# First row tiles in transfers of their own, first weights split behind the first roundings, and the next row's mean ahead of the last row's remainder

## What is computed

```python
xn = rmsnorm(x, norm1_g)            # x * rsqrt(mean(x*x) + EPS) * norm1_g
proj = xn @ w_in[0]                 # here: the q, k, v columns, 12 tiles of 128
qkv_c, new_buf = causal_conv(qkv, buf_qkv, conv_qkv_w)   # width 4, then SiLU
```

## Time and profile before

| | us |
|---|---|
| three runs, median | 1976.95 (1975.17 to 1980.42) |
| profiled execution, own time | 1980.5 |
| profiled execution, span | 1978.5 |

### The profile page before, as it was taken

One profiled execution on the slowest core, in us unless ns is written; L12 is line 12 of the kernel. 1 busy time (PEld: TensorE's weight loads), 2 busy tenths in 40 slices (PEclk: granted clock), 3 DMA queues, 4 the chain that ended last, 5 costly groups with the idle time before them and its releaser, 6 DMA issues. The chain is left out here.

```text
span 1978.5 us, 23341 instructions
## 1 busy us (share of the span) xinstructions
PE 1839.9 (93%) x10413; PEld 1727.8 (87%) x10413; DVE 724.1 (37%) x871; ACT 411.0 (21%) x590; POOL 98.1 (5%) x91
## 2 busy tenths in 40 slices
PE   5999799996799989979979989999999999999998
PEld 5999689995799989969977888989888898989887
DVE  5565566653311123222125333333333333333234
ACT  4233133330211011101113121111111111112021
POOL 1000233331000000000000000000000000000001
PEclk9999899998999989989999989999999999999999
DMA  5110100003021021121015011111111111111102
GB/s 175 33 33 22 47 1 1 1 7 85 12 77 40 0 54 44 32 65 37 27 46 188 1 44 43 54 32 54 32 54 32 47 39 43 43 43 43 43 11 96
DMA packets 109223, 88.08 MB, mean 45 GB/s; under 512 B 4010, under 2 KB 94839, under 8 KB 109132
## 3 DMA queue, kind: packets, MB, share of 16 engines
q1 hardware_dynamic: 109132, 86.72, 14.6%
HBM read 79.43 MB, written 7.28 MB: 44 GB/s over the span
## 5 line engine op out<-in xcount | busy, mean ns | idle before, releaser
L1891 PE MATMUL ps<-xn_hi,u_hi 128*128 128x384 f32 x768 | 258.7, 337 | 7.5 <-DVE u_lo L1773 5.5
L1891 PE MATMUL ps<-xn_lo,u_hi 128*128 128x384 f32 x768 | 258.2, 336 | 0.0
L1891 PE MATMUL ps<-xn_hi,u_lo 128*128 128x384 f32 x768 | 258.1, 336 | 0.0
L1900 PE MATMUL ps<-u_hi,hid_hi 128*128 128x512 f32 x576 | 226.5, 393 | 12.1 <-DVE hid_lo L1810 7.6
L1900 PE MATMUL ps<-u_hi,hid_lo 128*128 128x512 f32 x576 | 225.1, 391 | 0.0
L1900 PE MATMUL ps<-u_lo,hid_hi 128*128 128x512 f32 x576 | 224.9, 391 | 0.0
L1816 DVE TENSOR_TENSOR rows<-ps,rows 128x512 f32<-128x512 f32 x144 | 99.5, 691 | 245.0 <-PE ps L1900 245.0
L1891 PEld LDWEIGHTS ps<-xn_hi,u_hi 128*128 128x128 f32 x768 | 145.4, 189 | 8.2 <-DVE u_lo L1773 5.7
L196 PE MATMUL ps<-xn_hi,g_hi 128*128 128x384 f32 x384 | 130.4, 340 | 23.4 <-DVE g_lo L681 23.4
L196 PE MATMUL ps<-xn_hi,w_hi 128*128 128x384 f32 x384 | 130.7, 340 | 22.6 <-DVE w_lo L681 22.6
L1891 PEld LDWEIGHTS ps<-xn_lo,u_hi 128*128 128x128 f32 x768 | 145.6, 190 | 0.3
(11 more groups left out here) (250 smaller groups left out, 3029.4 us busy)
## 6 DMA issues: line engine op xcount, KB each, us to landing
w_raw<-in_w_up SPq DMA_DIRECT2D x32, 512.0 KB, 4.1
w_raw<-in_w_down SPq DMA_DIRECT2D x32, 512.0 KB, 3.8
w_raw<-in_w_in SPq DMA_DIRECT2D x28, 512.0 KB, 3.9
g_raw<-in_w_in SPq DMA_DIRECT2D x16, 512.0 KB, 4.5
rows<-in_x_prompt SPq DMA_DIRECT2D x9, 512.0 KB, 6.4
out<-out SPq DMA_DIRECT2D x9, 512.0 KB, 2.6
w_raw<-in_w_o SPq DMA_DIRECT2D x8, 512.0 KB, 4.4
rows<-in_x_prompt SPq DMA_DIRECT2D x2, 1024.0 KB, 10.1
```

The costliest lines, as they stand in the source:

```text
L1891: last = nc.tensor.matmul(ps[:, 3 * up_set(j) + g, 0:NW], y[:, j, w], x[:, k, x_at], start=(k == 0 and m == 0), stop=(k == KD - 1 and m == 2))
L1900: last = nc.tensor.matmul(ps[:, 6 + n % 2, :], x[:, k, r * P:(r + 1) * P], y[:, s, w], start=(k == 0 and m == 0), stop=(k == 3 and m == 2))
```

## The change

The rows' transfers are six instead of five: tiles 0, 1 and 2 each have their own. The order of issue becomes row tile 0, gain, row tile 1, the identity alone (`C_ONE` is column 128, `C_INC` column 256 of the table, so the transfer is half as large; the rest of the table, now from column 128, comes later as before), row tile 2, weight tile 0, row tiles 3 to 5, weight tile 1, and the rest as before. ACT's list has `split(0)` behind `square(3)` instead of ahead of `rounded(0)`, and `split(1)` behind `square(4)` instead of ahead of `rounded(1)`. DVE's list makes the mean of row tile r + 1 directly behind the scaling of row tile r, ahead of `left(r - 1)`; `rest(0)` moves from the round of r = 1 to that of r = 3, ahead of `left(2)`, and `rest(1)` from r = 2 to the end of the round of r = 4, behind `left(3)`. PE's and POOL's lists are as before.

```diff
-        X_GROUPS = ((0, 1), (1, 3), (3, 6), (6, 8), (8, 9))
+        X_GROUPS = ((0, 1), (1, 2), (2, 3), (3, 6), (6, 8), (8, 9))
...
                 load_x(0)
                 sp.dma_start(gain[:, :], norm1_g.to_broadcast([P, D])).then_inc(gain_in, 16)
-                sp.dma_start(self.con[:, 0:C_INC], table[:, 0:C_INC]).then_inc(ident_in, 16)
                 load_x(1)
+                sp.dma_start(self.con[:, 0:C_ONE], table[:, 0:C_ONE]).then_inc(ident_in, 16)
+                load_x(2)
                 load(0)
-                load_x(2)
+                load_x(3)
                 load(1)
-                load_x(3)
                 load_x(4)
+                load_x(5)
...
-                sp.dma_start(self.con[:, C_INC:C_END], table[:, C_INC:C_END]).then_inc(loaded, 16)
+                sp.dma_start(self.con[:, C_ONE:C_END], table[:, C_ONE:C_END]).then_inc(loaded, 16)
...
                 square(0)
                 square(1)
-                split(0)
                 rounded(0)
                 square(2)
-                split(1)
                 rounded(1)
                 square(3)
+                split(0)
                 rounded(2)
                 square(4)
+                split(1)
                 rounded(3)
...
+                mean_of(0)
                 for r in range(RT):
-                    mean_of(r)
                     scale(r)
-                    if r == 1:
+                    if r + 1 < RT:
+                        mean_of(r + 1)
+                    if r == 3:
                         rest(0)
-                    if r == 2:
-                        rest(1)
                     if r:
                         left(r - 1)
+                    if r == 4:
+                        rest(1)
                 left(RT - 1)
```

More of the change, by code:

```diff
@@ L226, in front @@
         v, alog, dtb, ea, gseq, egls = self.gate_tables()
-        x_in = self.sems(*(f"x_in{n}" for n in range(5)))
+        x_in = self.sems(*(f"x_in{n}" for n in range(6)))
         raw_ready = self.sems("raw_ready0", "raw_ready1")
```

## The result

The changed kernel takes **1981.05 us** (median of 12 executions, 1979.95 to 1981.99) where the kernel before, in the same comparison, takes 1976.72 (12 executions, 1975.17 to 1980.57): +4.3 us by the medians. The ratio is 1.0019 with a 95% interval of 1.001 to 1.0028, which is 3.8 us, the distance of the means (1981.10 and 1977.28). Medians and means part because the executions of before lie in groups, nine from 1975.2 to 1977.4 and three from 1980.0 to 1980.6. The change is a loss clear of noise, and under 0.3%. The forecast was 1981.5, +4.55.

A forecast was written before the change was run, and what follows sets the result against it. PE, busy 93% of the span, was taken as the bound. Waits of +2.85 us plus 1.7 for one clock fall gave +4.55: 1985.05 us against the profiled execution's 1980.5, a median of 1981.5, range 1976.7 to 1985.0.

The forecast's parts named there:

- The transfers: Start of the kernel: row tiles 3 to 5 still land at 15.6 us, bounds 15.2 and 16.1.
- the splitting: Weight splitting on ACT at the start: called hidden, as ACT finishes `rounded(1)` at about 14.3 us, then waits for row tile 3.
- The second weight tile: Ahead of `unit(1, 0)`: late `rest(1)` idles PE about 1.6 us; start at 32.8, early 1.8 us gone and 0.25 more.
- The wait for the square: Ahead of `unit(0, 1)`: `left(5)` queues behind a mean awaiting `square(7)`; PE idles 3.0 us, starting 2.45 us late at 41.15.
- The last turning: Turning of row tile 8: `left(6)` behind a mean awaiting `square(8)`; at 50.7, 2.85 us late, only 0.4 of it new.
- The clock: Ahead of `unit(0, 1)`: 3.0 us idle brings one fall to 1.2 GHz, costing 1.7 us; shorter idle times bring none.
- the step by idle length: PE's front idle times: 3.0 us judged by 3.75, 2.00 and 1.47 us neighbours, giving one fall; 1.6 and 1.4 none.
- The median: Whole kernel: 1981.5 us, from 1976.95 before, the profiled execution lying 3.5 us above that median.
- Rival B: Front of the kernel: the waits bite but the clock holds, +2.85 us or +1.9; chance 0.25.
- Rival C: More low clock ahead of `unit(1, 0)` or the last turning: +6.25 us with one more stretch, +7.95 with two; chance 0.17.
- D: The early start survives because `square(7)` comes early enough; last turning 1.8 us early; chance 0.05.
- E: Nothing reaches the end, 0 +- 1 us: late landing, waits in existing idle times, or a low-clock stretch falling away; chance 0.07.

## Why the prediction was right

**The transfers** did as worked out, slightly better. From the DMA views of the changed kernel (issue to landing), with SP's timeline:

```profile
rows<-in_x_prompt SPq DMA_DIRECT2D x1, 1536.0 KB, 11.5
...
2.11 0.43 SPq L277 DMA_DIRECT2D con<-in_table  x1
3.59 1.26 SPq L272 DMA_DIRECT2D rows<-in_x_prompt  x1
```

Row tiles 3 to 5 land at 3.59 + 11.5 = 15.1, not at 15.6 and just under the lower bound of 15.2. Hence the first product at 21.85 for 22.45. One remark fails: the splitting is not "hidden". It is so only in the sense that ACT then waits for row tile 3; with the old transfers and the same lists the first product was 1.9 us later.

**The second weight tile** was late by the mechanism named, with 1.77 us of idle time for 1.6. It came at 31.94, 0.85 us earlier than the 32.8 of the sum: 0.6 from the first product, the rest because PE was at full speed sooner (the turning of row tile 3, at 25.82, took 1.39 us for 1.60). That the first products run at the low clock is read from their pace, 0.32 us from start to start (24.54, 24.86, 25.18 in the changed kernel), as in the stretch at 1176.20; PEclk does not show it and reads 1.00 there:

```profile
22.00:26.50 4.50, 4.50 (x16) 4.40 (x17) 0.89 (x1) 0.00 (x0) 0.00 (x0) 1.00 0.88 290
```

Here the sum was mis-sized: it had the early start spent at this place, and 0.6 us of it was left.

**The wait for the square** is right to the place and the size: 3.00 us for 3.0, released by the remainder behind the mean. That the mean's place is the cause is shown by taking it back (-7 us against the changed kernel, the idle times down from 3.00 and 1.77 us to 1.23 and 0.15 us) and by making it alone (+4.7). The late weights add to it only where a mean holds `left(3)`. **The last turning** had an idle time of 1.21 us where 1.4 was expected.

**The clock** was right in number and wrong in place. One half-clock stretch was expected behind 3.00 us of idle time. In the first profile it stood behind 1.77 us, which the step had given none. It costs the same there, since nothing between the two takes it back: 51.43 is the forecast's 50.7 + 1.7 = 52.4 less the microsecond by which the first two terms were too large. So the step by idle length fails. Its neighbours were read rightly; these are the windows behind the idle times of 3.75 and 1.47 us in the kernel before:

```profile
1920.30:1923.80 3.50, 3.50 (x10) 2.71 (x10) 1.13 (x1) 0.00 (x0) 0.00 (x0) 0.51 0.48 150
1064.90:1068.00 3.10, 3.10 (x18) 2.71 (x19) 2.39 (x4) 2.01 (x4) 0.00 (x0) 1.00 1.08 342
```

But over all 14 profiles the clock fell behind the 3.75 us in 14, behind the 2.00 us in 13 and behind the 1.47 us in none, where it fell behind the 3.00 us in three of six and behind the 1.77 us in one of two: 3.00 us had it less often than 2.00 us. That idle times in the front bring it at all is likely: of the six profiles with one of 3.00 us four have a fall there, of the eight without none. What decides in the single case stays open.

The words of the Trainium skill (TensorE: Matmul & The Clock Gate, section HAM oscillation), that waits between bursts bring the lower clock back, hold for some of these idle times only; the waits for transfers in its example are mostly longer. What its section What's actually happening says of the start, that the number of slow matmuls differs from run to run, the runs now show: the turning of row tile 3 took 1.60 us and 1.04 us in the two profiles of before.

**The median** agrees to 0.5 us, in part by luck. The sum's own figure, 1985.05 for the profiled execution, was not met: it took 1981.2, next to its median, and the 3.5 us by which the first profile of before lay above its median belonged to that one execution. Taking them off was right. At the last turning the change costs 3.6 us against one profile of before and 4.2 against the other, where the sum has 4.55. The rest of the 4.3 may come from the stretch near 88 us, 1.6 us, that both profiles of the changed kernel have and one of two of the kernel before; the prediction had counted it as neutral. Rival B (the clock holds) does not fit: both profiles have a fall, and both differences are above its 2.85. Rival C needed a second stretch ahead of the last turning, and neither profile has one. D and E are refuted by the idle times.

## What to carry to other kernels

A step that is put ahead of another in one engine's list brings its wait with it: before moving it up, follow what it waits for through the lists of the other engines, for here a mean of 0.15 us held a remainder that PE needed, because its input stood on ACT behind the copy of a product that PE was still making. What gave the gain was to move the inputs (squares, whose data had landed and for which ACT had 7 us of idle time) and not the step that reads them. An earlier start is worth only what the next waits leave of it: 2.4 us at the first product was 0.6 us at the second weight tile and -3.2 us at the third place.

## What the runs showed of the hardware

The granted clock fell to 1.2 GHz behind the same idle time of 3.00 us in three profiles of six, once for 6.8 us and twice for about 3.4, and behind 1.77 us in one of two. It began 0.7 us before PE resumed in one profile, 0.3 us after in another and 1.4 us after in two. Behind 2.00 us of idle time late in the kernel, with a microsecond of transposes ahead of it, it fell in 13 profiles of 14.

PE can be at half clock without any idle time. In 6 of 14 profiles, in one of before and not in the other, there is such a stretch 36 to 37 us behind the last turning, worth 1.6 us (178.0 to 178.1 us to the next stage for 176.5). Another stands in all 14, 109 to 112 us behind the last turning. Both follow blocks of small products, in the kernel before:

```profile
81.51 2.17 PE L635 MATMUL ps<-con,ba_rows 16*128 16x8 f32 x18
155.89 2.06 PE L591 MATMUL ps<-con,square 128*128 128x1 f32 x18
```

That these blocks are the reason is not shown; no run leaves them out. In a kernel of 1977 us, two profiled executions of the same code spanned 1978.5 and 1973.6 us: effects of a few microseconds are read from places in the trace and from medians of many executions, not from two spans.
